# The last block's gate and up products of the feed-forward, from seven block products instead of eight

## The chip, the cores and the metric

The kernel runs on one core of one Trainium2 chip. The time is the device time of one execution in microseconds; the median of three runs is given, and the time of a kernel is compared with that of the kernel before on the same chip.

## The reference

One layer of a transformer trunk on x of 1 x 2048 x 1024 float32: RMS norm, one input projection, two attention branches (a sliding window with sinks, and a sparse one whose keys an indexer selects), a gated merge, an output projection, and then the feed-forward that the change touches:

```python
h2 = _rmsnorm(x, norm2_g)
ff = jax.nn.silu(h2 @ w_ffn_gate) * (h2 @ w_ffn_up)      # 1024 -> 2816
x = x + ff @ w_ffn_down                                  # 2816 -> 1024
return _rmsnorm(x, norm_f_g)
```

All is float32.

## The kernel before

The 2048 rows are worked in four blocks (`b` = 0 to 3) of 512. Activations of a block stand transposed in SBUF, as 8 tiles `k` of 128 features by 512 rows. First all four blocks are projected; then, block after block, come attention, the branch products, the output projection and the feed-forward.

A float32 product is made of three matmuls. Both operands are split into a high part (rounded to the matmul's type, `float32r`) and a low part (the rest), and high x high, high x low and low x high are added up in PSUM; function `three`, L1049 to L1051. For the feed-forward `H2hi`, `H2lo` hold the normed rows, and `WHI`, `WLO` the weights.

The weights come as a list of jobs (`JOBS`), each a tile of 512 KB: 128 columns of `w_ffn_gate` or `w_ffn_up` over all 8 `k`, or 256 rows by 512 columns of `w_ffn_down`. SyncE's queue loads them in this order into two buffers `WRAW`; it starts a load when the buffer's job of two before has been split. GpSimd splits them (`split`, L984 and L986): in two halves of 128x512, a TENSOR_SCALAR that makes `WHI` and a TENSOR_TENSOR that makes `WLO`; it waits for TensorE to be done with the job of two before. TensorE runs a job (`job`) as 24 matmuls of 512 columns into one PSUM bank.

The 22 column tiles of the feed-forward are taken in three parts of 8, 8 and 6 (`PARTS`). In a part each tile `i` has its gate job `("fg", b, i)` and its up job `("fu", b, i)`. ScalarE takes SiLU of the gate bank (`SL`, L1973), VectorE multiplies the up bank by it (L2525), ScalarE copies the product's high part (`FFhi`, L1977) and VectorE subtracts for the low part (`FFlo`, L2528). After the part's tiles its down projection (`rows`) takes `FFhi`, `FFlo` as weights, in two halves of the 1024 output columns, and VectorE adds its banks to `X1` (L2470). The first gate job of a block (`first_gate`, L1498 to L1500) works on two halves of 256 rows each, since the second half of `H2` is still being made (VectorE, `H2lo`, L2499); its matmuls have 256 columns.

Each engine executes its own list of instructions in order; semaphores tie the lists together. The order within each list is written out by hand, and no planner changes it. In blocks 0 to 2 attention work of the next block is put beside the feed-forward; in block 3 there is none.

## Time and profile before

| | us |
|---|---|
| median of three runs | 3200.31 (3200.3 to 3202.91) |
| span of the profiled execution, first to last instruction | 3196.7 |
| TensorE busy | 3156.0 (99%) |
| GpSimd busy | 2036.0 (64%) |
| VectorE busy | 1814.8 (57%) |
| ScalarE busy | 1420.8 (44%) |

The profile gives no time of its own for the profiled execution beside its span; the median of the runs is 3.6 us above the span, which is what lies around the instructions. A TensorE instruction's duration reaches beyond the start of the next, since matmuls are pipelined: what a matmul costs in a train is the distance from start to start. In a row of the timeline the first number is the start in us from the span's start, the second the duration in us.

### The profile page before, as it was taken

How to read it: one execution, taken by the hardware profiler on the slowest of the kernel's cores; microseconds unless marked ns; L12 is line 12 of the kernel's file. 1: busy time of each engine (PE TensorE's matmuls, PEld its weight loads, DVE VectorE, ACT ScalarE, POOL GpSimd, SP SyncE). 2: the span in 40 equal slices, each digit the busy share in tenths (PEclk: the TensorE clock that was granted, in tenths of full speed). 3: DMA queues.
4: the chain of work that ended last, by engine and by line, in shares of the span. 5: the costliest groups of instructions: out<-in, count | busy, mean ns of one | idle time of the engine just before them, and what ended most of it. 6: DMA issues, size and time to landing. Idle time of an engine off the chain costs nothing.

```text
span 3196.7 us, 44024 instructions
## 1 busy us (share of the span) xinstructions
PE 3156.0 (99%) x15678; PEld 2655.0 (83%) x15678; DVE 1814.8 (57%) x3706; ACT 1420.8 (44%) x2589; POOL 2036.0 (64%) x2201
## 2 busy tenths in 40 slices
PE   9999999999999999999999999999999999999998
PEld 7888888878878888888888888988888799888887
DVE  3335546537565545557666666967868689521111
ACT  3324435435473534337354534837655378320001
POOL 5666766665556666764666676366767922666676
PEclk9999999999999999999999999999999999999999
DMA  5765455355615333331533334163333500533332
GB/s 152 198 167 172 119 154 157 103 157 163 209 35 182 102 112 107 108 125 57 201 104 116 103 102 138 28 238 103 98 109 112 171 23 17 180 91 99 95 103 99
DMA packets 464201, 392.59 MB, mean 123 GB/s; under 512 B 29264, under 2 KB 394064, under 8 KB 463344
## 3 DMA queue, kind: packets, MB, share of 16 engines
q1 hardware_dynamic: 442544, 345.56, 36.0%
q10 hardware_dynamic: 21440, 44.22, 3.7%
q8 instruction: 126, 2.06, 0.3%
q14 instruction: 91, 0.75, 0.1%
HBM read 323.76 MB, written 62.81 MB: 121 GB/s over the span
## 4 chain that ended last, share of the span: by engine, by line
PE 92%; POOL 2%; ACT 2%; DVE 2%; issue 1%; DMA 1%; SPq 0%; POOLq 0%; ACTq 0%; DVEq 0%
PE BANK L1049 22%; PE BANK L1051 21%; PE BANK L1050 21%; PE LP L1049 4%; PE LP L1051 4%; PE LP L1050 4%; PE BANK L1330 3%; PE BANK L1355 2%; PE LP L1166 2%; PE LP L1165 2%; PE LP L1310 2%; PE LP L1311 2%; PE BANK L1357 2%; POOL WLO L986 1%; POOL WHI L984 1%
## 5 line engine op out<-in xcount | busy, mean ns | idle before, releaser
L986 POOL TENSOR_TENSOR WLO<-WRAW,WHI 128x512 fp32r<-128x512 f32 x912 | 1213.3, 1330 | 76.0
L984 POOL TENSOR_SCALAR WHI<-WRAW 128x512 fp32r<-128x512 f32 x912 | 639.6, 701 | 776.1 <-PE BANK L1051 622.1
L1049 PE MATMUL BANK<-H2hi,WHI 128*128 128x512 f32 x1376 | 538.7, 392 | 1.1 <-POOL WLO L986 1.1
L1050 PE MATMUL BANK<-H2lo,WHI 128*128 128x512 f32 x1376 | 535.9, 389 | 0.0
L1051 PE MATMUL BANK<-H2hi,WLO 128*128 128x512 f32 x1376 | 535.8, 389 | 0.0
L1049 PE MATMUL BANK<-HThi,WHI 128*128 128x512 f32 (+1 forms) x1024 | 405.1, 396 | 0.8 <-DVE QS L2044 0.5
L1050 PE MATMUL BANK<-HTlo,WHI 128*128 128x512 f32 (+1 forms) x1024 | 399.4, 390 | 0.0
L1051 PE MATMUL BANK<-HThi,WLO 128*128 128x512 f32 (+1 forms) x1024 | 399.3, 390 | 0.0
L1751 ACT ACTIVATE MASK<-SCD,THR 128x896 bf16<-128x896 f32 (+5 forms) x186 | 281.9, 1516 | 191.8 <-DVE THR L2104 164.6
L1051 PEld LDWEIGHTS BANK<-H2hi,WLO 128*128 128x128 f32 x1376 | 258.3, 188 | 54.4
L1049 PEld LDWEIGHTS BANK<-H2hi,WHI 128*128 128x128 f32 x1376 | 258.6, 188 | 53.3 <-issue 1.3
L1050 PEld LDWEIGHTS BANK<-H2lo,WHI 128*128 128x128 f32 x1376 | 258.6, 188 | 51.1
L2071 DVE TENSOR_SCALAR_CACHE_REDUCE MASK<-SCD,THR 128x640 bf16<-128x640 f32 (+2 forms) x192 | 278.1, 1486 | 3.4
L1739 ACT ACTIVATE RB<-LP 128x1024 f32<-128x1024 f32 (+7 forms) x176 | 143.4, 819 | 231.9 <-PE LP L1166 207.9
L2525 DVE TENSOR_TENSOR BANK<-BANK,SL 128x512 f32<-128x512 f32 x88 | 61.2, 696 | 325.7 <-PE BANK L1051 305.9
L2308 DVE SCALAR_TENSOR_TENSOR SCP<-RB,IW,SCP 128x1024 f32<-128x1024 f32 (+7 forms) x140 | 175.2, 1266 | 106.2 <-ACT RB L1739 105.2
L1051 PEld LDWEIGHTS BANK<-HThi,WLO 128*128 128x128 f32 (+1 forms) x1024 | 190.9, 186 | 42.8
L2237 DVE TENSOR_TENSOR PTlo<-BANK,PThi 128x512 fp32r<-128x512 f32 (+1 forms) x296 | 193.2, 659 | 57.5 <-ACT PThi L1680 56.4
L1049 PEld LDWEIGHTS BANK<-HThi,WHI 128*128 128x128 f32 (+1 forms) x1024 | 191.1, 187 | 38.8 <-issue 0.6
L1050 PEld LDWEIGHTS BANK<-HTlo,WHI 128*128 128x128 f32 (+1 forms) x1024 | 191.3, 187 | 36.9
L1633 ACT ACTIVATE LGb<-LGb,NMB 128x1024 f32<-128x1024 f32 (+7 forms) x192 | 174.1, 907 | 57.9 <-POOL NMB L905 54.8
L905 POOL TENSOR_SCALAR NMB<-MXB 128x1 f32<-128x1 f32 x112 | 32.6, 291 | 250.6 <-DVE MXB L2194 247.6
(314 smaller groups left out, 6457.6 us busy)
## 6 DMA issues: line engine op xcount, KB each, us to landing
WRAW<-in_w_in SPq DMA_DIRECT2D x124, 512.0 KB, 4.2
WRAW<-in_w_ffn_gate SPq DMA_DIRECT2D x88, 512.0 KB, 3.8
WRAW<-in_w_ffn_up SPq DMA_DIRECT2D x88, 512.0 KB, 3.8
WRAW<-in_w_ffn_down SPq DMA_DIRECT2D x88, 512.0 KB, 3.5
qsp<-QS SPq DMA_DIRECT2D x32, 512.0 KB, 5.8
WRAW<-in_w_out SPq DMA_DIRECT2D x32, 512.0 KB, 4.6
gates<-GS ACTq DMA_DIRECT2D x62, 256.0 KB, 2.2
...
```

The costliest lines, as they stand in the source:

```text
L984: nc.gpsimd.tensor_scalar(hi, raw, 1.0, 1.0, ALU.mult, ALU.mult).then_inc(w_hi, 1)
L986: nc.gpsimd.tensor_tensor(lo, raw, hi.bitcast(f32), ALU.subtract).then_inc(w_split, 1)
L1049: nc.tensor.matmul(dst, whi, mhi, start=first, stop=False)
L1050: nc.tensor.matmul(dst, whi, mlo, start=False, stop=False)
L1051: return nc.tensor.matmul(dst, wlo, mhi, start=False, stop=last)
L1330: last = nc.tensor.transpose(dst[:, 2 * e + h, :], probabilities(b, kind, p, h, t), IDENT[:, :])
L1633: nc.scalar.activation(lg, lg, ACT.Exp, bias=NMB[:, slot, 0:1], accum_out=(ES if s else RS)[:, j, h0:h0 + 1]).then_inc(probs, made(probs, ...
L1739: nc.scalar.activation(RB[:, g % 2, 0:w], logits(("idx",) + key)[:, 0:w], ACT.Relu).then_inc(relu_ready, made(relu_ready, key))
L1751: nc.scalar.activation(mask_of(b)[:, j, 0:w], found_at(b, j)[:, 0:w], ACT.Sign, bias=THR[:, j:j + 1].bitcast(f32), accum_out=CNT[:, j:j + ...
L2071: last = stepped(nc.vector.tensor_scalar(junk[:, j, 0:w], found_at(b, j)[:, 0:w], threshold(j), None, op, ALU.add, accum_out=CNT[:, j:j + 1]))
L2237: nc.vector.tensor_tensor(PTLO[b][r][:, 0:w, :], trans(key)[:, 0:w, :], PTHI[b][r][:, 0:w, :].bitcast(f32), ALU.subtract).then_inc(pt_read ...
L2308: ins = nc.vector.scalar_tensor_tensor(s, r, iw, s, ALU.mult, ALU.add)
```

## The change

Before, two neighbouring column tiles of gate (or of up) in the last block are two jobs: as blocks, 2 column tiles x 2 halves of `k` (4 tiles each) x 2 halves of the rows (256 each) is eight block products. Now they are one "quarter" `q` of the list `QUARTERS`, made from seven block products by Strassen's scheme in Winograd's form. Tiles 0 and 1 of the block stay as they were; tiles 2 to 21 are ten pairs, so there are 20 quarters, 6, 8 and 6 in the three parts, gate and up in turn.

A block product is 12 matmuls of 256 columns: 4 `k` times three. Its weight factor `m` (0 to 6) is one of three blocks of the loaded weights or one of four sums of them (`WSUM`, made by VectorE); its other factor is a block of `H2` or one of four sums of such blocks (`TF`, split into `TThi` and `TTlo`, made once, 128x1024 each). The high part of each weight factor (`FAhi`) is copied by ScalarE and its low part (`FAlo`) is subtracted by GpSimd, all seven. There is one buffer per `m`, which is written again when product `m` of the quarter before is done. The products go to three banks in the order P Q R Q P Q R; VectorE adds the parts into `SL` (gate) or `UPV` (up). The weights come as 1 MB for two tiles into two buffers `RAW`. Some semaphores elsewhere are joined into one another with the same waits.

The diff, without the joined semaphores:

```diff
+SEVEN = (NB - 1,)
+def paired(b, i):
+    return b in SEVEN and i >= 2
+QUARTERS = [(kind, b, i) for b in SEVEN for part in PARTS for i in part[::2] if paired(b, i) for kind in ("fg", "fu")]
+def quarters_of(b, part):
+    return [q for q, (_, c, i) in enumerate(QUARTERS) if c == b and i in part]
+BANKS = "PQRQPQR"
+LOWER = (0, 1, 2, 3, 4, 5, 6)
+def factor_of(q, m):
+    raw = RAW[q % 2]
+    return {0: raw[:, 0:4, 0, :], 4: raw[:, 4:8, 0, :], 5: raw[:, 4:8, 1, :], 1: WSUM[1][:, :, :],
+            2: WSUM[0][:, :, :], 3: WSUM[2][:, :, :], 6: WSUM[3][:, :, :]}[m]
+def sum_of(m):
+    return {1: 1, 2: 0, 3: 2, 6: 3}.get(m)
...
+def load_quarters(q):
+    kind, b, i = QUARTERS[q]
+    if q >= 2:
+        sp.wait_ge(factor_low, n(factor_low, (q - 2, 5)))
+        sp.wait_ge(factor_made, n(factor_made, ("sum", (q - 2, 3))))
+    made(raw_in[q % 2], q, 16)
+    w = io["w_ffn_gate" if kind == "fg" else "w_ffn_up"][0]
+    sp.dma_start(RAW[q % 2][:, :, :, :].rearrange("p k f c -> p k (f c)"), weights(w, range(KT), i * P, 2 * P)
+                 ).then_inc(raw_in[q % 2], 16)
+    if (kind, i) == ("fg", PARTS[-1][0] + 2):
+        load_gain(b)
...
+if key == ("fg", NB - 1, 1):
+    load_quarters(0)
+    load_quarters(1)
+for part in PARTS:
+    for at_ in range(3):
+        if key == ("fd", part[0], NB - 1, 0, at_):
+            qs = quarters_of(NB - 1, part)
+            for q in qs[:-2] if at_ == 0 else (qs[at_ - 3],):
+                if q + 2 < len(QUARTERS):
+                    load_quarters(q + 2)
...
+def lower_factors(q):
+    for m in LOWER:
+        pool.wait_ge(factor_hi, n(factor_hi, (q, m)))
+        nc.gpsimd.tensor_tensor(FAlo[m][:, :, :], factor_of(q, m), FAhi[m][:, :, :].bitcast(f32), ALU.subtract
+                                ).then_inc(factor_low, made(factor_low, (q, m)))
+def before_down(part, at_):
+    qs = quarters_of(NB - 1, part)
+    if at_ == 0:
+        for q in qs[0 if qs[0] == 0 else 1:-1]:
+            lower_factors(q)
+    elif at_ == 1:
+        lower_factors(qs[-1])
+    elif qs[-1] + 1 < len(QUARTERS):
+        lower_factors(qs[-1] + 1)
...
+def seven_products(q):
+    up = QUARTERS[q][0] == "fu"
+    release = dict(P=(part_summed, ("ff", (q, 0))) if up else (part_kept, ("silu", (q, 0))), Q=(part_summed, (q, "c21")), R=(part_summed, (q, "c12")))
+    dst = {}
+    for m, place in enumerate(BANKS):
+        if m < 3:
+            dst[place] = take(place, *release[place], ("seven", q, place))[:, 0:2 * P]
+        if m == 3:
+            pe.wait_ge(part_summed, n(part_summed, (q, "two")))
+        if m == 4:
+            pe.wait_ge(part_kept, n(part_kept, ("first", q)))
+        if m == 5:
+            pe.wait_ge(part_summed, n(part_summed, (q, "three")))
+        if m == 6:
+            pe.wait_ge(part_summed, n(part_summed, (q, "c22")))
+        pe.wait_ge(factor_low, n(factor_low, (q, m)))
+        t = {1: 1, 2: 0, 3: 2, 5: 3}.get(m)
+        if q == 0 and t is not None:
+            pe.wait_ge(factor_made, n(factor_made, ("turned low", t)))
+        for s in range(4):
+            if t is not None:
+                hi, lo = TThi[t][:, s, :], TTlo[t][:, s, :]
+            else:
+                k, r = s + (4 if m else 0), slice(2 * P if m == 6 else 0, 4 * P if m == 6 else 2 * P)
+                hi, lo = H2hi[:, k, r], H2lo[:, k, r]
+            d, end = dst[place], s == 3 and m > 3
+            nc.tensor.matmul(d, FAhi[m][:, s, :], hi, start=(m < 3 and s == 0), stop=False, skip_group_check=True)
+            nc.tensor.matmul(d, FAhi[m][:, s, :], lo, start=False, stop=False, skip_group_check=True)
+            last = nc.tensor.matmul(d, FAlo[m][:, s, :], hi, start=False, stop=end, skip_group_check=True)
+        last.then_inc(product_done, made(product_done, (q, m)))
...
+def high_factor(q, m):
+    if q:
+        act.wait_ge(product_done, n(product_done, (q - 1, m)))
+    if sum_of(m) is None:
+        act.wait_ge(raw_in[q % 2], n(raw_in[q % 2], q))
+    else:
+        act.wait_ge(factor_made, n(factor_made, ("sum", (q, sum_of(m)))))
+    nc.scalar.copy(FAhi[m][:, :, :], factor_of(q, m)).then_inc(factor_hi, made(factor_hi, (q, m)))
+def close_half(q):
+    kind, _, i = QUARTERS[q]
+    if kind == "fg":
+        act.wait_ge(part_summed, n(part_summed, (q, "c12")))
+        rest = SL[:, :, :].rearrange("p f r -> p (f r)")[:, 2 * P:]
+        nc.scalar.activation(rest, rest, ACT.Silu).then_inc(part_kept, made(part_kept, ("silu", (q, 1))))
+    else:
+        act.wait_ge(part_summed, n(part_summed, ("ff", (q, 1))))
+        s = i - [p for p in PARTS if i in p][0][0]
+        nc.scalar.copy(FFhi[:, s:s + 2, :], UPV[:, :, :]).then_inc(part_kept, made(part_kept, ("high", q)))
+def seven_steps(part):
+    qs = quarters_of(b, part)
+    for q in qs:
+        gate = QUARTERS[q][0] == "fg"
+        for m in range(7):
+            if m == 0:
+                act.wait_ge(product_done, n(product_done, (q, 0)))
+                if q >= 2:
+                    act.wait_ge(part_summed, n(part_summed, (q - 2, "c21")))
+                nc.scalar.copy(FIRSTP[q % 2][:, :], bank(("seven", q, "P"))[:, 0:2 * P]
+                               ).then_inc(part_kept, made(part_kept, ("first", q)))
+                if q > qs[0]:
+                    close_half(q - 1)
+            if q + 1 < len(QUARTERS):
+                high_factor(q + 1, m)
+            if m == 4 and gate:
+                act.wait_ge(product_done, n(product_done, (q, 4)))
+                if q:
+                    act.wait_ge(part_summed, n(part_summed, ("ff", (q - 1, 1))))
+                else:
+                    act.wait_ge(ff_ready, n(ff_ready, (b, 1)))
+                nc.scalar.activation(SL[:, 0, 0:2 * P], bank(("seven", q, "P"))[:, 0:2 * P], ACT.Silu
+                                     ).then_inc(part_kept, made(part_kept, ("silu", (q, 0))))
+    if qs:
+        close_half(qs[-1])
...
+if b in SEVEN and i == 0:
+    for t in range(4):
+        act.wait_ge(factor_made, n(factor_made, ("turned", t)))
+        nc.scalar.copy(TThi[t][:, :, :], TF[t][:, :, :]).then_inc(factor_hi, made(factor_hi, ("turned", t)))
+    for m in range(7):
+        high_factor(0, m)
...
+def form_turned():
+    def whole(t, k, r):
+        c = slice(2 * P * r, 2 * P * (r + 1))
+        dve.wait_ge(h_split, n(h_split, (b, 1, r, 2 * k + 1)))
+        nc.vector.tensor_tensor(TF[t][:, :, :], H2hi[:, 4 * k:4 * k + 4, c].bitcast(f32),
+                                H2lo[:, 4 * k:4 * k + 4, c].bitcast(f32), ALU.add
+                                ).then_inc(factor_made, made(factor_made, ("turned", ("whole", t))))
+    def less(t, a, b_):
+        dve.wait_ge(factor_made, n(factor_made, ("turned", a)))
+        dve.wait_ge(factor_made, n(factor_made, ("turned", b_)))
+        i, j = (x[1] if type(x) is tuple else x for x in (a, b_))
+        nc.vector.tensor_tensor(TF[t][:, :, :], TF[i][:, :, :], TF[j][:, :, :], ALU.subtract
+                                ).then_inc(factor_made, made(factor_made, ("turned", t)))
+    whole(2, 0, 1)
+    whole(0, 0, 0)
+    whole(1, 1, 1)
+    whole(3, 1, 0)
+    less(0, ("whole", 2), ("whole", 0))
+    less(2, ("whole", 1), ("whole", 2))
+    less(1, ("whole", 1), 0)
+    less(3, ("whole", 3), 1)
+def sum_weights(q, k):
+    raw = RAW[q % 2]
+    a11, a12, a21, a22 = raw[:, 0:4, 0, :], raw[:, 4:8, 0, :], raw[:, 0:4, 1, :], raw[:, 4:8, 1, :]
+    dve.wait_ge(raw_in[q % 2], n(raw_in[q % 2], q))
+    if q:
+        dve.wait_ge(factor_low, n(factor_low, (q - 1, (2, 2, 3, 6)[k])))
+    if k in (1, 3):
+        dve.wait_ge(factor_made, n(factor_made, ("sum", (q, {1: 0, 3: 1}[k]))))
+    a, b_, op = {0: (a21, a22, ALU.add), 2: (a11, a21, ALU.subtract), 1: (WSUM[0][:, :, :], a11, ALU.subtract),
+                 3: (a12, WSUM[1][:, :, :], ALU.subtract)}[k]
+    nc.vector.tensor_tensor(WSUM[k][:, :, :], a, b_, op).then_inc(factor_made, made(factor_made, ("sum", (q, k))))
+def add_part(q, what):
+    up = UPV if QUARTERS[q][0] == "fu" else SL
+    place, m, other, to = dict(two=("Q", 1, FIRSTP[q % 2], TWO[:, :]), three=("Q", 3, FIRSTP[q % 2], THREE[:, :]),
+                               c22=("R", 2, THREE, up[:, 1, 2 * P:]), c21=("Q", 5, FIRSTP[q % 2], up[:, 1, 0:2 * P]),
+                               c12=("R", 6, TWO, up[:, 0, 2 * P:]))[what]
+    dve.wait_ge(product_done, n(product_done, (q, m)))
+    if what == "two":
+        dve.wait_ge(part_kept, n(part_kept, ("first", q)))
+    if what in ("c22", "c12"):
+        dve.wait_ge(part_summed, n(part_summed, (q, "three" if what == "c22" else "two")))
+    if q and what in ("two", "three"):
+        dve.wait_ge(part_summed, n(part_summed, (q - 1, "c12" if what == "two" else "c22")))
+    if what == "c22" and up is UPV and q > 1:
+        dve.wait_ge(ff_split, n(ff_split, (b, QUARTERS[q - 2][2] + 1)))
+    if what == "c22" and up is SL:
+        dve.wait_ge(part_summed if q else ff_ready, n(part_summed, ("ff", (q - 1, 1))) if q else n(ff_ready, (b, 1)))
+    nc.vector.tensor_tensor(to, bank(("seven", q, place))[:, 0:2 * P], other[:, :], ALU.add
+                            ).then_inc(part_summed, made(part_summed, (q, what)))
+def multiply(q, rest):
+    dve.wait_ge(part_kept, n(part_kept, ("silu", (q - 1, rest))))
+    if rest:
+        dve.wait_ge(part_summed, n(part_summed, (q, "c12")))
+        up, gate = (t[:, :, :].rearrange("p f r -> p (f r)")[:, 2 * P:] for t in (UPV, SL))
+        nc.vector.tensor_tensor(up, up, gate, ALU.mult).then_inc(part_summed, made(part_summed, ("ff", (q, 1))))
+    else:
+        dve.wait_ge(product_done, n(product_done, (q, 4)))
+        nc.vector.tensor_tensor(UPV[:, 0, 0:2 * P], bank(("seven", q, "P"))[:, 0:2 * P], SL[:, 0, 0:2 * P], ALU.mult
+                                ).then_inc(part_summed, made(part_summed, ("ff", (q, 0))))
+def low_ff(q):
+    i = QUARTERS[q][2]
+    dve.wait_ge(part_kept, n(part_kept, ("high", q)))
+    for f in range(2):
+        s = i + f - [p for p in PARTS if i in p][0][0]
+        nc.vector.tensor_tensor(FFlo[:, s, :], UPV[:, f, :], FFhi[:, s, :].bitcast(f32), ALU.subtract
+                                ).then_inc(ff_split, made(ff_split, (b, i + f)))
+def seven_steps(part):
+    qs = quarters_of(b, part)
+    for q in qs:
+        up, more = QUARTERS[q][0] == "fu", q + 1 < len(QUARTERS)
+        for k in (0, 2) if more else ():
+            sum_weights(q + 1, k)
+        add_part(q, "two")
+        for k in (1, 3) if more else ():
+            sum_weights(q + 1, k)
+        if q > qs[0] and not up:
+            low_ff(q - 1)
+        add_part(q, "three")
+        add_part(q, "c22")
+        if up:
+            multiply(q, 0)
+        add_part(q, "c21")
+        add_part(q, "c12")
+        if up:
+            multiply(q, 1)
+    if qs:
+        low_ff(qs[-1])
...
+if b in SEVEN and i == 0:
+    for k in (0, 2, 1, 3):
+        sum_weights(0, k)
+    for t in range(4):
+        dve.wait_ge(factor_hi, n(factor_hi, ("turned", t)))
+        nc.vector.tensor_tensor(TTlo[t][:, :, :], TF[t][:, :, :], TThi[t][:, :, :].bitcast(f32), ALU.subtract
```

The other lines: TensorE, ScalarE and VectorE skip the paired tiles in their loops over a part and run `seven_products(q)` or `seven_steps(part)` after them, ahead of the down projection; VectorE runs `form_turned()` ahead of the first part's loop; GpSimd runs `before_down(part, at_)` ahead of the splitting of the down projection's first three jobs; the PSUM banks are taken in turn, P from 4 and 0, Q from 5 and 1, R from 6 and 2.

## Rows read from the trace of the kernel before

**Rows 1.** The page, busy time and share of the span by engine.

```profile
PE 3156.0 (99%) x15678; PEld 2655.0 (83%) x15678; DVE 1814.8 (57%) x3706; ACT 1420.8 (44%) x2589; POOL 2036.0 (64%) x2201
```

**Rows 2.** Window of the last block's feed-forward: length, TensorE busy, clock, DMA share.

```profile
2834.50:3189.00 354.50, 353.81 (x1562) 1.00 0.31 94
```

**Rows 3.** Timeline of ScalarE, SiLU of two gate tiles in a row.

```profile
2845.63 0.60 ACT L1973 ACTIVATE SL<-BANK 128x512 f32<-128x512 f32 x1 [4.12 <-PE BANK L1051]
...
2856.51 0.60 ACT L1973 ACTIVATE SL<-BANK 128x512 f32<-128x512 f32 x1 [4.12 <-PE BANK L1051]
```

**Rows 4.** Timeline of TensorE, last block, first gate job's end, next job's start.

```profile
2832.96 0.35 PE L1498 MATMUL BANK<-H2hi,WHI 128*128 128x256 f32 x1
2833.15 0.28 PE L1499 MATMUL BANK<-H2lo,WHI 128*128 128x256 f32 x1
...
2833.63 0.28 PE L1500 MATMUL BANK<-H2hi,WLO 128*128 128x256 f32 x1
...
2834.40 0.28 PE L1500 MATMUL BANK<-H2hi,WLO 128*128 128x256 f32 x1
2834.53 0.39 PE L1049 MATMUL BANK<-H2hi,WHI 128*128 128x512 f32 x1
```

**Rows 5.** Timeline of GpSimd at the kernel's end, a train of four.

```profile
3182.74 5.05 POOL L1008 TENSOR_TENSOR XH<-X,GFB 128x512 f32<-128x512 f32 x4
```

**Rows 6.** Timeline: VectorE's 512-element operation alone, then against GpSimd's.

```profile
602.51 0.75 DVE L2308 SCALAR_TENSOR_TENSOR SCP<-RB,IW,SCP 128x512 f32<-128x512 f32 x1 [0.68 <-ACT RB L1739]
...
615.22 1.30 POOL L986 TENSOR_TENSOR WLO<-WRAW,WHI 128x512 fp32r<-128x512 f32 x1
...
615.43 1.63 DVE L2308 SCALAR_TENSOR_TENSOR SCP<-RB,IW,SCP 128x512 f32<-128x512 f32 x1 [0.78 <-ACT RB L1739]
```

**Rows 7.** Timelines, 836 to 843 us, of both; and 256 elements from PSUM, grouped.

```profile
836.07 7.12 DVE L2396 TENSOR_TENSOR TABA<-TABA,BANDM 128x256 f32<-128x256 f32 x8
...
839.49 1.51 DVE L2396 TENSOR_TENSOR TABA<-TABA,BANDM 128x256 f32<-128x256 f32 x1
...
840.92 0.83 DVE L2396 TENSOR_TENSOR TABA<-TABA,BANDM 128x256 f32<-128x256 f32 x1
...
839.38 1.34 POOL L986 TENSOR_TENSOR WLO<-WRAW,WHI 128x512 fp32r<-128x512 f32 x1
...
841.57 1.34 POOL L986 TENSOR_TENSOR WLO<-WRAW,WHI 128x512 fp32r<-128x512 f32 x1
...
L2237 DVE TENSOR_TENSOR PTlo<-BANK,PThi 128x256 fp32r<-128x256 f32 x32 | 13.4, 419 | 3.2 <-ACT PThi L1680 3.2
```

**Rows 8.** Timelines, 66 to 72 us: VectorE's four subtractions and GpSimd's beside the last.

```profile
66.92 3.98 DVE L2364 TENSOR_TENSOR AKSlo<-KAT,AKShi 64x512 fp32r<-64x512 f32 x4 [3.56 <-ACT AKShi L1824]
...
70.45 1.61 POOL L986 TENSOR_TENSOR WLO<-WRAW,WHI 128x512 fp32r<-128x512 f32 x1
```

**Rows 9.** ScalarE's copy in SBUF (ns min/median/max); VectorE's 1024 elements, two in a row.

```profile
L1705 ACT CAST OThi<-OTA x16: 607/622/647, 933.3 to 2728.7; 128x512 fp32r<-128x512 f32 x16
...
1517.10 2.53 DVE L2435 SCALAR_TENSOR_TENSOR X<-X,SS,GFB 128x1024 f32<-128x1024 f32 x2
```

**Rows 10.** Timelines of VectorE and GpSimd at the start of the stage.

```profile
2830.43 3.22 DVE L2499 SCALAR_TENSOR_TENSOR H2lo<-LP,G,H2hi 128x256 fp32r<-128x256 f32 x8 [2.16 <-ACT H2hi L1965]
...
2851.07 0.70 DVE L2525 TENSOR_TENSOR BANK<-BANK,SL 128x512 f32<-128x512 f32 x1 [8.84 <-PE BANK L1051]
...
2834.85 0.62 POOL L984 TENSOR_SCALAR WHI<-WRAW 128x512 fp32r<-128x512 f32 x1 [4.11 <-PE BANK L1500]
...
2840.32 0.62 POOL L984 TENSOR_SCALAR WHI<-WRAW 128x512 fp32r<-128x512 f32 x1 [1.52 <-PE BANK L1051]
...
2842.28 0.62 POOL L984 TENSOR_SCALAR WHI<-WRAW 128x512 fp32r<-128x512 f32 x1
```

**Rows 11.** The loads of the last block's gate weights, us to landing at the end.

```profile
WRAW<-in_w_ffn_gate SPq DMA_DIRECT2D x11, 512.0 KB, 3.8
```

**Rows 12.** Window at the kernel's end; the clock follows POOL's busy time.

```profile
3192.00:3196.70 4.70, 0.00 (x0) 0.00 (x0) 0.00 (x0) 0.00 (x0) 0.00 (x0) 0.58 0.79 315
```

88 lines of the change are left out of this document (62 added, 26 removed).

## The prediction

> **What bounds the kernel now.** I read the page's busy times first: TensorE is busy 99% of the span [rows 1]. Then the windows of the stage that changes, the last block's feed-forward: from 2834.5 to 3189.0 us TensorE is busy 353.81 of 354.50 us at full clock [rows 2]. No engine is waited for there, so the stage's length is its matmuls' spacing. Third, ScalarE's timeline: the activation of one gate tile follows the last by 10.88 us [rows 3]. That is a tile's gate job and up job, 48 matmuls of 512 columns, 0.2267 us each. Two neighbouring tiles of one kind (gate or up), which the change does as one "quarter", cost the same 48 matmuls, 10.88 us; there are 20 quarters, 217.6 us. Only what happens to these counts. The reordered semaphores elsewhere leave every wait as it was: 0.
>
> **TensorE's part.** A quarter becomes 7 products of 4 x 3 = 12 matmuls of 256 columns: 84. Two of them cost a little more than one of 512. The first gate job already runs such matmuls: four steps from 2833.15 to 2833.63 take 0.48 us [rows 4], and steps between 0.11 and 0.12 us hold elsewhere in that job: 0.118 us. 84 x 0.118 = 9.91 us. So TensorE alone would save 0.97 us a quarter (19.4 us in all), 9% and not the 12.5% of the arithmetic. A wait that is already met costs next to nothing (2834.40 to 2834.53, with the waits of a new job between, is 0.13 [rows 4]).
>
> **GpSimd's part.** Until now it forms high and low parts of two jobs per 10.88 us: four pairs of 1.96 us [rows 10], 7.8 us. Now ScalarE copies the high parts and GpSimd only subtracts: 7 low parts, 512 elements each. A train of four such takes 5.05 us [rows 5] and a single one 1.30 [rows 6], so start to start (5.05 - 1.30) / 3 = 1.25 us: 8.8 us a quarter. Alone that fits into 9.91 us, with 11% to spare. ScalarE has 7 copies of 0.62 us [rows 9] and under 2 us of the rest: 6 of 9.9 us, hidden.
>
> **VectorE's part, and the collision.** A quarter adds on VectorE 4 weight sums (512 elements, both inputs in SBUF), 5 additions from PSUM (256 elements, 0.42 us [rows 7]), and per pair of quarters 2 low parts of FF (512) and a product of 768 elements, both inputs in SBUF again. By itself: 4 x 0.61 + 5 x 0.45 + 1.2 = 5.9 us, which fits too. But these SBUF-to-SBUF operations don't run beside GpSimd's. A 512-element operation of VectorE takes 0.75 us while GpSimd is idle and 1.63 us when it begins just after a GpSimd subtraction [rows 6]: it ends 0.54 us after that one's end. The eight 256-element additions in [rows 7] took 7.12 us instead of about 8 x 0.35 = 2.8, one for each operation of GpSimd. Four subtractions of [rows 8] took 3.98 us instead of 2.5, and the GpSimd subtraction that met the last took 1.61 instead of 1.30.
>
> What does it cost GpSimd, which has only 11% to spare? In [rows 7] GpSimd's cycle of two operations is 841.57 - 839.38 = 2.19 us with two 256-element operations of VectorE put in, against 1.96 undisturbed [rows 10]: 0.12 each. By its length (256 elements more, 0.27 us) a 512-element one adds 0.39; the other bound is the 0.32 of [rows 8]; 768 adds 0.65. I take 0.39. A quarter's turn is then 8.8 + 4 x 0.39 + (2 x 0.39 + 0.65) / 2 = 11.1 us, above TensorE's 9.9 and just above the 10.88 of now.
>
> The Trainium skill states this as a rule ("SBUF — State Buffer", Who interferes with whom): a VectorE instruction with two SBUF inputs and a GpSimd instruction that reads SBUF exclude each other for the whole instruction. The waits of [rows 6] agree with it; the overlap at the ends in [rows 7] makes the price smaller than whole instructions.
>
> The chain between the engines adds to it. Follow a gate quarter from the end of its seventh low part (0). The sum k=3 of the next quarter waits for that part; GpSimd has begun its next by then, so the sum ends at 1.75, the two FF low parts behind it at 3.4 and 5.05 (each behind one of GpSimd), the addition "three" at 5.5. Product 5 waits for "three": 5.5 to 6.9, product 6 to 8.3; then ScalarE's copy (9.0) and GpSimd, with a sum in between: the seventh low part of the next quarter ends at 10.5. In the following up quarter the first low part waits for ScalarE, which closes the gate half first, and the second for sum k=1: about 1.3 us of GpSimd idle; its seventh ends at 21.8. Next pair: 33.9 and 44.9. That is 11.5 us a quarter. After a real wait TensorE's next step is longer (2832.96 to 2833.15, 0.19 us [rows 4]); that is inside the figure. So + 0.62 us a quarter.
>
> **The start.** VectorE ends H2lo at 2833.65 [rows 10]. Then come 8 operations of 1024 elements to form the turned sums (two such took 2.53 us [rows 9]), 9.9 us alone; they collide with the weight splitting of the gate and up jobs of tile 1 at 2834.85 and 2840.32 (3.9 us each), one behind the other: end about 2850 instead of 2843.6, and the splitting ends near 2849, which may hold the up job by 0.6 us. Then VectorE does tile 0's product and low part (2.0 us with ScalarE's copy), ScalarE four copies of 1024 (1.1 each) and the seven high parts (0.62 each); the first low part is at 2858.4, while TensorE is free for quarter 0 at 2851 (VectorE's wait for tile 1's up job ends at 2851.07 [rows 10]). VectorE's four turned low parts alternate with GpSimd's: second 2860.8, third 2863.1; "two" comes behind tile 1's work and two sums of the next quarter, 2867; products 3 to 6 end by 2873. The two jobs replaced would have ended at 2861.8: + 11 us. A product waits over 7 us there; at the kernel's end, after the last matmul (3188.3 us), the granted clock averages 0.58 of full from 3192.0 on [rows 12], so it has fallen from 2.4 to 1.2 GHz within it. Some of the first products may so run at 1.2 GHz; as they wait for factors, I count 0. If form_turned and the factors did not collide, the start costs 5; if the clock matters, 14.
>
> **The rest.** Each down projection now has the splitting of its first two weights among the quarters, 3.9 us of GpSimd once a part; in parts 2 and 3 the first quarter finds its factors ready (made during the down projection, where TensorE is busy 44 us), which gives about as much back: 0, bounds - 4 and + 6 in all. The loads: 1 MB a quarter; 512 KB land in 3.8 us [rows 11], so at most 7.6; a load is released about 10 us before its first use. Hidden with 2.4 us of margin. SP's queue holds these loads ahead of the down weights, which are wanted 10 us later: 0. The end of the kernel is untouched.
>
> **Sum.** 19 quarters x 0.62 = + 11.8, start and first quarter + 11, rest 0: + 23 us on a span of 3196.7, or 3219.7. The runs' median lies 3.6 above that span, so 3223.
>
> **Rivals.**
> A, TensorE-bound as intended (faster): each collision costs GpSimd only the 0.12 of [rows 7]; 8.8 + 5.5 x 0.12 = 9.5 us, under 9.9. Then 20 x (10.88 - 10.1) = 15.6 saved, start 5: 3190. For it: GpSimd mostly keeps its pace in [rows 7]. Against: the 1.61 of [rows 8].
> B, a draw: GpSimd's turn at the low bound, 8.8 + 4 x 0.32 + 0.57 = 10.65, other waits hidden: - 4.6, start + 8: 3204.
> C, full exclusion, slower still: whole operations add, 8.8 + 4 x 0.61 + 1.05 = 12.3 us a quarter, + 28, start + 12: 3240. It decides from the point where GpSimd's turn passes 10.88 us. For it: the waits of [rows 6 to 8]. Against: the two operations put into the cycle of [rows 7] cost it less than their lengths. The rule of the Trainium skill ("SBUF — State Buffer", Who interferes with whom), taken literally, is this rival.
>
> **How the numbers follow.** Forecast 0.5 (3209 to 3236), A 0.2, B 0.15, C 0.15. The measurement can tell 0.2%, 6.4 us, from no change. Faster is A with a little of B, 0.22; same most of B, 0.14; slower 0.64. The range 3190 to 3240 leaves out about one in ten on each side.
>
> **What would show it.** TensorE's matmuls of 256 columns 0.118 us apart within a product, with idle gaps before products 3, 5 and 0; these waits end on VectorE's additions or GpSimd's low parts. GpSimd's subtractions with a mean of 1.5 us or more, busy nearly all through the quarters, VectorE's sums at 1.2 us or more instead of 0.7. Twenty quarters of 11.5 us. A gap of some 7 us at 2851. It is wrong if TensorE shows no gaps (A), or if a wait ends on a DMA.

## The result and the profile after

The changed kernel takes 3224.86 us, the median of 4 runs (3223.53 to 3228.09), beside 3200.51 (3200.3 to 3202.91, 4 runs) of the kernel before: ratio 1.0075, 95% interval 1.0061 to 1.0089. It is slower, by 24.3 us; forecast was + 23. The profiled execution took 3228.09 us around a span of 3225.7; it is the slowest of the four. Its span lies 29.0 us above that of before, and the accounts below are of these 29.0.

The page of the kernel after, busy time by engine, answers to [rows 1], and the stage's window to [rows 2]: columns are length, then busy time and instructions of PE, PEld, DVE, ACT, POOL, then granted clock, DMA share and GB/s.

```profile
PE 3152.7 (98%) x16398; PEld 2683.5 (83%) x16398; DVE 1992.2 (62%) x3898; ACT 1509.2 (47%) x2743; POOL 2106.3 (65%) x2181
```

```profile
2834.50:3189.00 354.50, 321.64 (x2166) 298.05 (x2166) 217.52 (x253) 115.33 (x199) 297.27 (x220) 0.98 0.27 86
```

TensorE has lost what it had in [rows 2]: it stands still for 32.9 of 354.5 us. VectorE's time beside it grew from 48 to 218 us.

Where a quarter ends shows in VectorE's timeline, at the last addition of each, "c12". A middle part of the stage (columns: start, us, engine, line, operation, tiles, and in brackets the idle time before with its releaser):

```profile
2997.50 0.42 DVE L2755 TENSOR_TENSOR UPV<-BANK,TWO 128x256 f32<-128x256 f32 x1 [1.02 <-PE BANK L1622]
...
3011.05 0.42 DVE L2755 TENSOR_TENSOR SL<-LP,TWO 128x256 f32<-128x256 f32 x1 [1.01 <-PE LP L1622]
...
3021.14 0.42 DVE L2755 TENSOR_TENSOR UPV<-BANK,TWO 128x256 f32<-128x256 f32 x1 [1.01 <-PE BANK L1622]
...
3034.79 0.42 DVE L2755 TENSOR_TENSOR SL<-LP,TWO 128x256 f32<-128x256 f32 x1 [1.01 <-PE LP L1622]
```

A gate quarter takes 13.55 to 13.65 us and an up quarter 10.08: 23.7 a pair, where four jobs took 2 x 10.88 = 21.76 [rows 3]. The up quarter is TensorE-bound, 84 x 0.12. TensorE's timeline shows the 3.5 us of the gate quarter as two gaps and the longer step behind each:

```profile
2998.73 0.28 PE L1620 MATMUL LP<-TThi,FAhi 128*128 128x256 f32 x1
2998.85 0.28 PE L1621 MATMUL LP<-TTlo,FAhi 128*128 128x256 f32 x1
...
3001.49 0.28 PE L1622 MATMUL LP<-TThi,FAlo 128*128 128x256 f32 x1
3003.08 0.39 PE L1620 MATMUL LP<-TThi,FAhi 128*128 128x256 f32 x1 [1.30 <-DVE TWO L2755]
...
3005.93 0.28 PE L1622 MATMUL LP<-H2hi,FAlo 128*128 128x256 f32 x1
3007.88 0.39 PE L1620 MATMUL LP<-TThi,FAhi 128*128 128x256 f32 x1 [1.67 <-DVE THREE L2755]
```

Before product 3 it waits for "two", before product 5 for "three". VectorE's timeline of the same quarter says why they are late, and GpSimd's what was beside them:

```profile
2998.03 1.27 DVE L2764 TENSOR_TENSOR UPV<-UPV,SL 128x768 f32<-128x768 f32 x1
2999.22 3.47 DVE L2736 TENSOR_TENSOR WSUM<-RAW 128x512 f32<-128x512 f32 x2
3002.61 0.41 DVE L2755 TENSOR_TENSOR TWO<-LP,FIRSTP 128x256 f32<-128x256 f32 x1
3002.95 1.43 DVE L2736 TENSOR_TENSOR WSUM<-WSUM,RAW 128x512 f32<-128x512 f32 x1
3004.51 0.69 DVE L2736 TENSOR_TENSOR WSUM<-RAW,WSUM 128x512 f32<-128x512 f32 x1
3005.12 2.37 DVE L2776 TENSOR_TENSOR FFlo<-UPV,FFhi 128x512 fp32r<-128x512 f32 x2
3007.41 0.41 DVE L2755 TENSOR_TENSOR THREE<-LP,FIRSTP 128x256 f32<-128x256 f32 x1
```

```profile
3002.10 1.73 POOL L1087 TENSOR_TENSOR FAlo<-RAW,FAhi 128x512 fp32r<-128x512 f32 x1
3005.16 4.71 POOL L1087 TENSOR_TENSOR FAlo<-WSUM,FAhi 128x512 fp32r<-128x512 f32 x3 [1.33 <-ACT FAhi L2100]
3009.84 2.55 POOL L1087 TENSOR_TENSOR FAlo<-RAW,FAhi 128x512 fp32r<-128x512 f32 x2
```

The two sums take 1.7 us each while GpSimd subtracts. The one at 3004.51 takes 0.69: GpSimd is idle there, until ScalarE has copied the high part of the sum at 3002.95. That sum was slow because of GpSimd in turn, and so a ring closes, GpSimd, VectorE's sum, ScalarE, GpSimd, once a quarter. Grouped over the stage (busy us, mean ns of one; idle us before them), both engines are slow at what they do in SBUF, and VectorE's 256-element additions from PSUM are not (the last line):

```profile
L1087 POOL TENSOR_TENSOR FAlo<-WSUM,FAhi 128x512 fp32r<-128x512 f32 x80 | 118.3, 1500 | 17.4 <-ACT FAhi L2100 17.4
L1087 POOL TENSOR_TENSOR FAlo<-RAW,FAhi 128x512 fp32r<-128x512 f32 x60 | 91.7, 1543 | 19.1 <-ACT FAhi L2100 18.8
...
L2736 DVE TENSOR_TENSOR WSUM<-RAW 128x512 f32<-128x512 f32 x40 | 61.6, 1579 | 0.0
L2736 DVE TENSOR_TENSOR WSUM<-WSUM,RAW 128x512 f32<-128x512 f32 x20 | 26.2, 1312 | 0.0
L2776 DVE TENSOR_TENSOR FFlo<-UPV,FFhi 128x512 fp32r<-128x512 f32 x20 | 26.1, 1347 | 3.4 <-ACT FFhi L2112 3.4
...
L2755 DVE TENSOR_TENSOR SL<-LP,FIRSTP 128x256 f32<-128x256 f32 x10 | 4.2, 425 | 17.1 <-PE LP L1622 17.1
```

The start of the stage, timelines of GpSimd and VectorE (answering to [rows 10]) and TensorE's two waits:

```profile
2835.91 7.22 POOL L1051 TENSOR_SCALAR WHI<-WRAW 128x512 fp32r<-128x512 f32 x1 [4.10 <-PE BANK L1589]
2843.22 2.11 POOL L1053 TENSOR_TENSOR WLO<-WRAW,WHI 128x512 fp32r<-128x512 f32 x1
...
2834.63 4.62 DVE L2705 TENSOR_TENSOR TF<-H2hi,H2lo 128x1024 f32<-128x1024 f32 x4
2839.17 5.03 DVE L2713 TENSOR_TENSOR TF<-TF,TF 128x1024 f32<-128x1024 f32 x4
...
2845.47 0.47 PE L1138 MATMUL BANK<-H2hi,WHI 128*128 128x512 f32 x1 [4.26 <-POOL WLO L1053]
...
2847.50 0.63 PE L1138 MATMUL BANK<-H2hi,WHI 128*128 128x512 f32 x1
...
2865.52 0.39 PE L1620 MATMUL LP<-TThi,FAhi 128*128 128x256 f32 x1 [2.98 <-DVE TWO L2755]
```

One high part, 0.62 us in [rows 10], took 7.22: GpSimd got in only beside the last of the eight turned sums, while VectorE ran them at full speed, 1.15 us each. TensorE waited 4.26 us in the middle of tile 1's gate job, and the matmul at 2847.50 is one of eight that are 0.41 to 0.43 us apart from start to start. The windows show the granted clock behind both waits, 0.57 and 0.50 of 2.4 GHz, so 1.2 GHz for most of the first window and all of the second. The last two windows lie at two later waits of 2.27 us, and the clock was at 1.2 GHz there too:

```profile
2847.50:2850.00 2.50, 2.50 (x8) 1.96 (x7) 2.50 (x3) 2.24 (x3) 2.42 (x3) 0.57 0.01 3
...
2867.50:2870.00 2.50, 2.50 (x14) 2.50 (x13) 1.77 (x3) 1.07 (x3) 2.50 (x3) 0.50 0.70 245
...
2918.00:2921.30 3.30, 3.11 (x14) 3.11 (x15) 0.70 (x3) 0.14 (x1) 3.30 (x3) 0.50 0.00 0
3170.60:3173.90 3.30, 3.30 (x18) 3.30 (x17) 0.42 (x1) 0.62 (x1) 3.30 (x4) 0.50 0.41 135
```

So the 29.0 us: 1.06 ahead of the stage (the first gate job's end is that much later in this execution; in a profile of the same code up to there, turned_apart below, it is 1.2 us earlier than in the profile before, so this is scatter); 10.05 until quarter 0's end (2873.06 against 2861.95); 5.4, 6.7 and 5.1 in the other 5, 7 and 5 quarters of parts 1 to 3; some 0.7 where parts meet.

The pace of 23.7 us is that of the pairs in mid-part. The last pair of each part takes 25.7, 25.4 and 25.8 us: in its gate quarter GpSimd also splits the first weights of the down projection (5.4 us, from 2911.81), and the wait before product 5 is 2.27 us. At this wait the clock fell in parts 1 and 3 and not in part 2, and by the pairs' lengths that cost no more than 0.4 us. The first gate quarter of parts 2 and 3 has no gap at all.

### The profile page after: what moved, and what is told of

Its sections match the earlier page's. It is cut to its first block and busy times, and to the rows that moved or that the text cites. A ratio compares the mean times of both kernels' runs of the same rounds, so it can differ in the third digit from the quotient of the medians.

```text
span 3225.7 us, 46150 instructions
## 1 busy us (share of the span) xinstructions
PE 3152.7 (98%) x16398; PEld 2683.5 (83%) x16398; DVE 1992.2 (62%) x3898; ACT 1509.2 (47%) x2743; POOL 2106.3 (65%) x2181
## 5 line engine op out<-in xcount | busy, mean ns | idle before, releaser
L1053 POOL TENSOR_TENSOR WLO<-WRAW,WHI 128x512 fp32r<-128x512 f32 x832 | 1115.1, 1340 | 69.4
L1051 POOL TENSOR_SCALAR WHI<-WRAW 128x512 fp32r<-128x512 f32 x832 | 599.8, 721 | 703.6 <-PE BANK L1140 551.6
L1138 PE MATMUL BANK<-H2hi,WHI 128*128 128x512 f32 x1056 | 415.0, 393 | 5.5 <-POOL WLO L1053 5.5
L1139 PE MATMUL BANK<-H2lo,WHI 128*128 128x512 f32 x1056 | 412.1, 390 | 0.0
L1140 PE MATMUL BANK<-H2hi,WLO 128*128 128x512 f32 x1056 | 411.9, 390 | 0.0
L1138 PEld LDWEIGHTS BANK<-H2hi,WHI 128*128 128x128 f32 x1056 | 198.8, 188 | 45.7 <-issue 6.0
L1140 PEld LDWEIGHTS BANK<-H2hi,WLO 128*128 128x128 f32 x1056 | 198.6, 188 | 42.1
L1139 PEld LDWEIGHTS BANK<-H2lo,WHI 128*128 128x128 f32 x1056 | 198.9, 188 | 38.8
L1805 ACT CAST PThi<-BANK 128x512 fp32r<-128x512 f32 (+1 forms) x296 | 164.2, 560 | 49.9 <-PE BANK L1419 47.2
```

The costliest lines, as they stand in the source:

```text
L1051: nc.gpsimd.tensor_scalar(hi, raw, 1.0, 1.0, ALU.mult, ALU.mult).then_inc(w_hi, 1)
L1053: nc.gpsimd.tensor_tensor(lo, raw, hi.bitcast(f32), ALU.subtract).then_inc(w_split, 1)
L1138: nc.tensor.matmul(dst, whi, mhi, start=first, stop=False)
L1139: nc.tensor.matmul(dst, whi, mlo, start=False, stop=False)
L1140: return nc.tensor.matmul(dst, wlo, mhi, start=False, stop=last)
L1805: nc.scalar.copy(PTHI[b][r][:, 0:w, :], trans(key)[:, 0:w, :]).then_inc(pt_hi, made(pt_hi, key))
```

## The experiments

Theory 1: in SBUF, GpSimd's subtractions and VectorE's two-input operations take turns, and this sets the quarter. Theory 2: VectorE's queue is simply too long ahead of "two" and "three", whatever GpSimd does. Theory 3: GpSimd has simply too many subtractions, whoever is beside it. The runs were made on more than one chip, so each is compared by its ratio to the kernel before on the same chip; that kernel took 3198.2 to 3199.2 us there.

**free_port.** The second input of the weight sums from quarter 1 on and of FF's low parts comes from a PSUM bank; their values are other ones, counts, lengths and order the same.

```diff
@@ sum_weights
+                    if q:
+                        b_ = in_tiles(BANK[3])
                     nc.vector.tensor_tensor(WSUM[k][:, :, :], a, b_, op)...
@@ low_ff
-    tensor_tensor(FFlo[:, s, :], UPV[:, f, :], FFhi...
+    tensor_tensor(FFlo[:, s, :], BANK[3][:, :], FFhi...
```

> Takes the collision away and nothing else: the weight sums of the quarters (from the second on) and the FF low parts read one of their two inputs from a PSUM bank (bank 3, which holds old values) instead of SBUF; same engine, order, element count and waits. What is left out: the right values of these sums and low parts. Theory 1 (VectorE's SBUF-to-SBUF operations and GpSimd's subtractions shut each other out): sums and low parts fall from 1.2 to 1.6 us to 0.7, GpSimd's seven subtractions from a mean of 1.52 to 1.29, the gaps of TensorE before products 3 and 5 go, a gate quarter falls from 13.65 to about 10.2 us; ten of them give back some 33 us: 3190 to 3197. Theory 2 (VectorE's queue is simply too long in front of the additions 'two' and 'three', whatever the port does): each gap keeps half or more, 3208 or later. Theory 3 (seven subtractions are too much for GpSimd by themselves, 8.8 us and the waits for ScalarE): gate quarters not under 11.4 us, 3205 or later.

Measured: 3191.01 us (3190.53 to 3192.23) beside 3199.13 of the kernel before, ratio 0.9975 [0.9965, 0.9984], as theory 1 expected. From the fourth on every quarter takes 10.08 us, and TensorE has no gap in them; the wait of 4.26 us at the start stays. GpSimd's and VectorE's groups:

```profile
L1087 POOL TENSOR_TENSOR FAlo<-WSUM,FAhi 128x512 fp32r<-128x512 f32 x80 | 110.8, 1406 | 3.4 <-ACT FAhi L2100 3.4
L1087 POOL TENSOR_TENSOR FAlo<-RAW,FAhi 128x512 fp32r<-128x512 f32 x60 | 78.0, 1313 | 27.6 <-ACT FAhi L2100 27.6
...
L2738 DVE TENSOR_TENSOR WSUM<-RAW,BANK 128x512 f32<-128x512 f32 x57 | 37.5, 682 | 8.2 <-POOL FAlo L1087 6.2
L2778 DVE TENSOR_TENSOR FFlo<-BANK,FFhi 128x512 fp32r<-128x512 f32 x20 | 12.8, 684 | 3.3 <-ACT FFhi L2112 3.3
```

The sums fall from 1579 to 682 ns with the same elements in the same places of the queue. It is not that PSUM is faster to read: the sum at 3004.51 above, with both inputs in SBUF and GpSimd idle, took 0.69 us. Theory 3 falls: the same 140 subtractions fit. Theory 2 falls as well, since the queue has the same operations in the same order. The changed kernel is 24.3 us above the kernel before and this one 8.1 below it, so some 32 us are one source operand of 96 instructions. The Trainium skill ("SBUF — State Buffer", Who interferes with whom) says that a VectorE instruction with two SBUF inputs contends with a GpSimd instruction that reads SBUF, and that one with at most one SBUF input does not, outside VectorE's 2-port modes; the 1579 and 682 ns agree.

**low_ff_late.** FF's low parts move behind "c21".

```diff
-                        if q > qs[0] and not up:
-                            low_ff(q - 1)
                         add_part(q, "three")
...
                         add_part(q, "c21")
+                        if q > qs[0] and not up:
+                            low_ff(q - 1)
```

> Keeps every collision, changes only VectorE's order: the two FF low parts of a gate quarter come behind the addition c21 instead of ahead of 'three'. Theories 1 and 2: the gap before product 5 (1.67 to 2.27 us in each gate quarter after a part's first, seven of them) goes, the one before product 3 (1.3 to 1.4) stays: 12 to 16 us less, 3209 to 3213. If the low parts, moved, collide with the next quarter's sums, part comes back in the gap before product 3: up to 3220. Theory 3: no change, 3225.

Measured: 3223.78 (3221.61 to 3225.51), 1.0076 [1.0061, 1.0091]: as the changed kernel. The number of theories 1 and 2 is missed, and that of theory 3, no change, came true; free_port had already ruled theory 3 out as a cause. TensorE's timeline of a pair and the next gate quarter:

```profile
3001.22 0.39 PE L1620 MATMUL LP<-TThi,FAhi 128*128 128x256 f32 x1 [1.30 <-DVE TWO L2755]
...
3013.13 0.39 PE L1620 MATMUL BANK<-TThi,FAhi 128*128 128x256 f32 x1 [1.57 <-DVE TWO L2755]
...
3024.89 0.38 PE L1620 MATMUL LP<-TThi,FAhi 128*128 128x256 f32 x1 [1.42 <-DVE TWO L2755]
```

The gap before product 5 is gone, one before product 3 of the up quarter has come, and the pair still takes 3024.89 - 3001.22 = 23.67 us. A gap's place is set by the order, the pair's length by the ring; what was wrong in theory 1's number was to take a moved gap for a lost one.

**lows_shared.** GpSimd keeps four of the seven low parts, VectorE takes three.

```diff
-        LOWER = (0, 1, 2, 3, 4, 5, 6)
+        LOWER = (0, 1, 2, 3)
...
                         add_part(q, "two")
+                        lower(q, 6)
...
                         add_part(q, "c21")
+                        lower(q + 1, 4)
                         add_part(q, "c12")
+                        lower(q + 1, 5)
```

> Low parts 4, 5 and 6 move from GpSimd to VectorE (behind c21, behind c12, behind 'two'); GpSimd keeps 0 to 3. Theory 1: GpSimd holds the port 5.0 instead of 8.8 us a quarter, VectorE adds 3 x 0.4 to 0.6; turn of about 8 us, under TensorE's 9.9, but VectorE has ten operations in line, so some of the gaps stay: gate quarters 10.5 to 12 us, 3200 to 3212. Theory 2: VectorE's queue gets three more operations (2 us) and the gaps grow: 3230 or later. Theory 3: GpSimd is relieved of 43%: the gaps go, 3190 to 3196.

Measured: 3230.95 (3230.07 to 3233.73), 1.01 [1.0085, 1.0115], slower than the change. Theories 1 and 3 missed, and theory 2's number, 3230 or later, came true, though not by gaps that grew. A mid-part pair takes 24.5 us. GpSimd's subtractions fall to 1432 and 1440 ns and its load by 3 of 7, and VectorE's queue is now the longer chain: TensorE waits once a pair, 2.61 us, where the change waits 1.30 and 1.67. But behind this wait its clock fell to 1.2 GHz (the window):

```profile
3011.77 0.39 PE L1624 MATMUL LP<-TThi,FAhi 128*128 128x256 f32 x1 [2.61 <-DVE THREE L2766]
...
3012.70:3016.00 3.30, 3.30 (x18) 3.30 (x17) 1.02 (x2) 0.62 (x1) 1.06 (x1) 0.50 0.00 0
```

Fifteen steps there took 0.21 us in place of 0.12, which with the two half-slowed ones beside them makes 1.5 us a pair. Without them the pair would be at 23.0 (an estimate from these two numbers), below the change's 23.7: in mid-part it is the clock, not the sharing, that makes this kernel slower than the change. No run tried the sharing with the clock kept up.

**shared_reordered.** lows_shared, with low_ff behind "c21" as in low_ff_late, and the first seven-product pair one pair of tiles later (`i >= 4`).

> As lows_shared (low parts 4, 5, 6 on VectorE), with the FF low parts behind c21 and with the seven products from tile 4 on. lows_shared was slower (3231): its pair of quarters took 24.5 us, with a gap of 2.6 us before product 5, since VectorE's queue had ten SBUF-to-SBUF operations a quarter. If VectorE's place in line is what matters there, the gap before product 5 goes and a pair takes 21 to 22 us: 3203 to 3210. If VectorE is full (its 16 operations of a pair with GpSimd's eight between them), the gap moves to product 3 and a pair stays at 23 us or more: 3213 to 3220.

Measured: 3217.81 (3216.3 to 3220.74), 1.0058 [1.0044, 1.0072]. In mid-part a pair takes 21.55 us (3003.43 to 3024.98), so the order in VectorE's queue made the wait of lows_shared, as the first case expected. The time is that of the second case, 3213 to 3220: the last pair of parts 1 and 2 waits 2.44 and 3.95, then 2.53 and 3.93 us, for "two", with the clock at 1.2 GHz behind the longer ones. Against start_later (1.0064) the sharing gains nothing clear of the scatter.

**start_later.** The change with `i >= 4` alone in place of `i >= 2`: 18 quarters.

```diff
-            return b in SEVEN and i >= 2
+            return b in SEVEN and i >= 4
```

> The seven products begin with tile 4 instead of tile 2 (9 pairs, 18 quarters); the turned sums are still formed beside tile 0. Theory: the start's cost (about 10 us up to the end of the first quarter, from the turned sums and the first factors being late) hides behind tiles 2 and 3, and one pair is spared its 1.9 us; but the gate job of tile 1 still waits 4.3 us for its weights, whose split is shut out by the turned sums: 3224.9 - 10 + 4.5 - 2 = 3217, between 3213 and 3219. Rival: the start's cost is that of any first quarter, whenever it comes: 3223.

Measured: 3219.76 (3217.3 to 3222.4), 1.0064 [1.0049, 1.0079], just outside the expected 3213 to 3219. That is 20.6 us above the kernel before in place of 24.3, and the intervals of the two ratios overlap, so the gain rests on the trace. The wait of 2.98 us shrinks to 0.46, the one of 4.26 at tile 1's gate job stays, and the quarters still cost 23.7 us a pair.

**turned_psum.** The eight turned sums take one input from PSUM (other values, same lengths). Of the later four, two get a wait for the sum just before, which the last one had already.

```diff
-    tensor_tensor(TF[t][:, :, :], H2hi[...], H2lo[...], ALU.add
+    tensor_tensor(TF[t][:, :, :], H2hi[...], LP[1][...], ALU.add
...
+                        if t:
+                            dve.wait_ge(factor_made, n(factor_made, ("turned", {2: 0, 1: 2, 3: 1}[t])))
-    tensor_tensor(TF[t][:, :, :], TF[i][:, :, :], TF[j][:, :, :], ALU.subtract
+    tensor_tensor(TF[t][:, :, :], TF[i][:, :, :], LP[1][...], ALU.subtract
```

> The eight operations that form the turned sums read one of their two inputs from PSUM (banks 6 and 7, old values) instead of SBUF. Left out: the right values of these sums. In the changed kernel GpSimd's high part of tile 1's gate weights took 7.22 us instead of 0.62 during them, and TensorE waited 4.26 us for that job. Theory 1 (the port): that operation takes 0.62 us again and the wait goes; but VectorE's own chain to the first quarter's factors (turned low parts, tile 1, two sums, 'two') is as long as before, so the first quarter ends nearly where it did: 3221 to 3225 in all, the 4.3 us turning up as a longer wait ahead of quarter 0. Rival (the weights came late from memory, or GpSimd waited for something else): the 7 us stay.

Measured: 3221.55 (3220.56 to 3222.96), 1.0067 [1.0052, 1.0083], as expected. GpSimd and VectorE; the first two operations of GpSimd lie beside the four sums that have no added wait:

```profile
2837.01 0.63 POOL L1051 TENSOR_SCALAR WHI<-WRAW 128x512 fp32r<-128x512 f32 x1 [4.11 <-PE BANK L1589]
2837.72 1.30 POOL L1053 TENSOR_TENSOR WLO<-WRAW,WHI 128x512 fp32r<-128x512 f32 x1
...
2835.73 4.61 DVE L2705 TENSOR_TENSOR TF<-H2hi,LP 128x1024 f32<-128x1024 f32 x4
```

7.22 us are 0.63 again and the wait of 4.26 is gone. Part of it comes back as four waits in the first quarter (0.46, 0.52, 0.56, 2.09 us). The rival, weights that came late from memory, falls.

**turned_apart.** Operands as in the change, but each turned sum waits for the one just before it.

```diff
+                    def behind(what):
+                        if formed:
+                            dve.wait_ge(factor_made, n(factor_made, ("turned", formed[-1])))
+                        formed.append(what)
```

> The changed kernel with one more wait ahead of each of the eight turned sums: on the sum just before it on VectorE. Data, order and operands stay. In the changed kernel GpSimd's high part at the start took 7.22 us and ended only beside the eighth sum, the only one that waits for the sum just before it; this asks whether it is the back-to-back issue that keeps GpSimd out. Theory 1 (a stream of such instructions holds the port from one to the next, and a wait on the predecessor opens it): GpSimd's high part takes under 2 us, TensorE's wait of 4.26 us at tile 1's gate job falls under 0.5 and the half clock behind it goes; the eight sums take about 1 us longer, and part of it comes back as waits in the first quarter, as in turned_psum: 3219 to 3223. Theory 2 (the kind of instruction alone keeps GpSimd out, however it is issued): the 7.2 us and the wait of 4.26 stay, 3225 to 3226.

Measured: 3224.24 (3222.82 to 3226.15), 1.008 [1.0066, 1.0093]: the mechanism as theory 1 said, the time not (3219 to 3223); it lies between the two expectations. GpSimd, VectorE, TensorE:

```profile
2833.68 0.62 POOL L1051 TENSOR_SCALAR WHI<-WRAW 128x512 fp32r<-128x512 f32 x1 [4.11 <-PE BANK L1589]
2834.38 2.14 POOL L1053 TENSOR_TENSOR WLO<-WRAW,WHI 128x512 fp32r<-128x512 f32 x1
...
2832.40 6.75 DVE L2713 TENSOR_TENSOR TF<-H2hi,H2lo 128x1024 f32<-128x1024 f32 x4
2839.29 7.43 DVE L2722 TENSOR_TENSOR TF<-TF,TF 128x1024 f32<-128x1024 f32 x4
...
2847.91 0.50 PE L1138 MATMUL BANK<-H2hi,WHI 128*128 128x512 f32 x1 [0.71 <-POOL WLO L1053]
2854.82 0.55 PE L1620 MATMUL LP<-H2hi,FAhi 128*128 128x256 f32 x1 [3.89 <-POOL FAlo L1087]
```

With the waits the engines alternate one for one and GpSimd is no longer kept out, but the sums take 14.3 us instead of 9.6, not the 1 us more that was expected (this profile lies 2.2 us ahead of the change's at the start). They hold up tile 0's product behind them, so ScalarE's turned high parts, so quarter 0's first low part: the wait of 4.26 us has become one of 0.71 and one of 3.89 in quarter 0, and behind the latter the clock was at 1.2 GHz again (0.50 from 2855.0 to 2860.0).

**sums_from_psum.** A complete kernel. ScalarE copies the blocks a21 and a11 of the weight tile into two PSUM banks that are free in mid-part; three of the four sums read one input there, in 12 of the 18 quarters. low_ff goes behind "c21", and `i >= 4`.

```diff
+                    act.wait_ge(factor_made, n(factor_made, ("sum", (q - 1, 1))))
+                    nc.scalar.copy(in_tiles(BANK[3]), raw[:, 0:4, 1, :])...
+                    nc.scalar.copy(in_tiles(LOW4[3]), raw[:, 0:4, 0, :])...
...
+                    if freed(q) and k != 3:
+                        a, b_ = {0: (b3, a22), 2: (a11, b3), 1: (WSUM[0][:, :, :], b7)}[k]
```

> A complete kernel: ScalarE copies two of the four weight blocks into PSUM banks 3 and 7, which the quarters leave free, and VectorE takes three of the four weight sums (k = 0, 2, 1) with one input from there, wherever the quarter two before lies in the same part (12 of 18 quarters); GpSimd keeps all seven low parts; FF low parts behind c21; seven products from tile 4 on. Theory 1: port turn 8.8 + 0.39 + 0.72 = 9.9 us where freed, about TensorE's 10.1; the other 6 quarters as before, 11.8. 12 x (10.88 - 10.2) - 6 x 0.95 = 2.5 gained, start 4.5 + up to 3 lost: 3199 to 3206, some 15 under start_later. Theory 2 or 3: as start_later and low_ff_late, 3218 to 3220, plus ScalarE's 1.2 us a quarter if that is in the way.

Measured: 3197.65 (3195.62 to 3199.54) beside 3199.16, 0.9995 [0.9986, 1.0003], the same as the kernel before and 1.4 us better than theory 1 expected. start_later is the kernel to hold it against, 20.6 us above before and this one 1.5 below: 22 us for the place of one input (low_ff behind "c21" moved nothing in low_ff_late). A pair in mid-part takes 20.2 us, against 21.76 before. The wait of 4.27 us at tile 1's gate job is still there, with the low clock behind it.

**sums_psum_apart.** sums_from_psum with the `behind` of turned_apart.

> sums_from_psum (3197.65 beside 3199.16 of the kernel before) with the same extra waits on the sum just before, for the eight turned sums alone. sums_from_psum still had TensorE's wait of 4.27 us at tile 1's gate job, and some 2 us of half clock behind it; its first seven-product quarter comes two pairs of tiles later, so a slower chain of eight sums costs nothing there. Theory 1: both go, 3191.5 to 3194.5, which is faster than the kernel before by 0.15 to 0.25%. Theory 2: nothing moves, 3197 to 3198.5.

Measured: 3193.43 (3192.89 to 3195.77, 11 runs) beside 3198.22, 0.9982 [0.9973, 0.9991], as expected, and faster than the kernel before and than the change. sums_from_psum was 1.5 us below the kernel before and this one is 4.8; the intervals of these two ratios touch, the traces differ clearly. Here the slower chain of sums has two more tiles of time, and at the start only waits of 0.68, 0.80 and, in its first quarter, 1.63 us are left. The window of the stage and VectorE's sums:

```profile
2834.50:3189.00 354.50, 341.75 (x2205) 310.96 (x2203) 179.76 (x249) 129.68 (x233) 302.83 (x245) 1.00 0.28 92
```

```profile
L2766 DVE TENSOR_TENSOR WSUM<-BANK,RAW 128x512 f32<-128x512 f32 x14 | 9.5, 678 | 0.9 <-issue 0.9
L2766 DVE TENSOR_TENSOR WSUM<-RAW,WSUM 128x512 f32<-128x512 f32 x18 | 20.2, 1123 | 6.5 <-POOL FAlo L1094 4.5
```

## Why the prediction was right, point by point

**TensorE's part.** 84 x 0.118 = 9.91 was forecast; the pace is 0.12, so 10.08. Right but for 0.17 us, and free_port shows the whole stage at it. That it lies below 10.88 is why a version of this change can gain.

**GpSimd's part and the collision.** The mechanism was right, and free_port isolates it. The turn without the collision was put at 8.8 us; the collision at 0.39 for each 512-element operation. Where both engines alternate, a subtraction starts every 1.69 us (3000.41 to 3002.10), 0.44 above the 1.25 of [rows 5]: the price was about right. But a quarter has only 210.0 / 20 = 10.5 us of subtractions (1500 and 1543 ns; at least 1.5 us was forecast), against 11.1 for the turn, since some of VectorE's operations fell into GpSimd's idle time, as the one at 3004.51 did. The sums' 1579 and 1312 ns were forecast as 1.2 or more.

**The chain.** 11.5 us a quarter forecast, 11.85 measured (23.7 / 2), though as 13.6 and 10.1 in turn and not as twenty alike. The step that was short is GpSimd's idle time: the chain gave it 1.3 us once a pair, in the up quarter; it is 1.33 in both, since in each the second low part waits for ScalarE's copy of a sum that VectorE could only form between subtractions. 2 x 10.5 + 2 x 1.33 = 23.7. So the turn was put too high and the idle time too low, and 11.5 came as near as it did partly because the two errors cancel. Over 19 quarters the cost is 17.2 + 0.7 us instead of 11.8. The row quoted for the longer step after a wait (2832.96) has no wait ahead of it; behind real waits the step is 0.22 us (2865.52 to 2865.74). The gaps lie where they were forecast before products 3 and 5, not before product 0; and, but for one of 0.80 us, only in gate quarters, where the product of 768 elements and the FF low parts stand in VectorE's queue as well. low_ff_late shows that this matters for the place alone.

**The start.** + 11 forecast, 10.05 measured, but by another way: this is the step that failed, and that its number fits is luck. The forecast let form_turned and the splitting take turns, with 0.6 us of TensorE's time for it and the gap at quarter 0. They did not take turns: GpSimd was shut out. From the timelines: 4.4 us at tile 1's gate job, 1.6 of low clock behind it, 3.1 before product 3 of quarter 0, 1.6 of low clock behind that, less 0.8 for the shorter quarter: 9.9. The gap of 7 us at 2851 isn't there: its work was done while TensorE waited earlier. turned_psum and turned_apart show the cause from two sides. The clock, taken at 0, costs 3.2 us, the 3 of the bound "if the clock matters, 14"; a shorter wait than forecast made up for it.

**The rest.** Loads, SP's queue and the end of the kernel cost nothing, as forecast; no wait of TensorE in the stage ends on a DMA, though a 1 MB load takes 5.4 us to land. The splitting among the quarters and the first quarters of parts 2 and 3 were put at 0 together. Against the pace of mid-part the three last pairs cost 5.8 us more, and the two first gate quarters, without gaps and so at 10.1 in place of 13.6, give 7 back: right.

**The sum.** 10.05 + 17.2 + 0.7 is 28 against 23, in an execution 3.2 us above its median; the medians differ by 24.3. The forecast also put 3.6 us between span and time; where both are on record for one execution they lie 1.7 to 2.4 us apart, so the profiled execution of before was a short one. So 3223 is nearer to 3224.86 than its terms deserve: the quarters were put 6 us too low, and the scatter of the profiled executions lies between. Rival A (TensorE-bound, 3190) needs the port free: free_port is it, at 3191. Rival B (3204) had GpSimd's turn nearly right, 10.65 against 10.5; it fails on its "other waits hidden", the 1.33 us of idle time a quarter, and on the start. Rival C, whole exclusion, is refuted for the pace of the quarters: it needs 1.25 + 0.61 = 1.86 us from one alternating subtraction to the next, and that took 1.69, so the operations overlap at their ends; and a quarter took 11.85 us with the idle time in it, where C has 12.3 without. Only at the start was GpSimd kept out wholly, and for longer than C has it. The Trainium skill's rule ("SBUF — State Buffer", Who interferes with whom) so names the right pairs of instructions, and a price from its letter is too high where both alternate (1.86 against 1.69) and far too low where one streams (7.22 us).
